# Base added into the accumulators by VectorE between two expert steps, expert bias opens them, embedding gate in eight pieces of 256 columns in odd steps

## The reference

```python
x = _layernorm(DEEPNORM_ALPHA * x + mix, ln1_g[layer], ln1_b[layer], dt)
moe_out = moe(x.reshape(bsz * seq, D_MODEL), router_w[layer], router_b[layer], expert_w_gu[layer],
              expert_b_gu[layer], expert_w_down[layer], expert_b_down[layer]).reshape(bsz, seq, D_MODEL)
ple = jax.nn.sigmoid(x @ ple_gate_w[layer]) * (p[layer] @ ple_proj_w[layer])
x = _layernorm(DEEPNORM_ALPHA * x + moe_out + ple, ln2_g[layer], ln2_b[layer], dt)
...
# in moe, for each expert e of a token's four, with weight g:
#   gate, up = x @ w_gu[e] + b_gu[e];  h = (min(up) + 1) * gate * sigmoid(1.702 * gate);  y += g * (h @ w_down[e] + b_down[e])
```

## Time and profile before

| | us |
|---|---|
| median of 3 runs | 1730.97 (1730.95 to 1731.19) |
| profiled execution, first to last instruction (span) | 1728.9 |
| median of the runs less that span | 2.1 |
| TensorE busy | 1701.2 |
| VectorE busy | 582.5 |
| ScalarE busy | 265.1 |
| mean rate of all transfers | 313 GB/s |

### The profile page before, as it was taken

The page is one execution under the profiler, slowest core; times in us unless marked ns, Lnnn a source line. Parts: engine busy times, 40 slices in busy tenths (PEclk is TensorE's granted clock), DMA queues, the critical chain, the costliest instruction groups (busy, mean ns, idle before and its releaser), DMA issues.

```text
span 1728.9 us, 24503 instructions
## 1 busy us (share of the span) xinstructions
PE 1701.2 (98%) x10237; PEld 1000.7 (58%) x10237; DVE 582.5 (34%) x1085; ACT 265.1 (15%) x455; POOL 26.3 (2%) x37
## 2 busy tenths in 40 slices
PE   9999999999999999999999999999999999999998
PEld 8787888888643433333333343433333338998885
DVE  4685368454331111111111111112121135544643
ACT  1323115002011111101010010101010122112211
POOL 1000000100000000000000000000000000000000
PEclk9999999999999999999999999999999999999999
DMA  9564332545799999999999999999999997443231
GB/s 343 196 257 159 146 123 100 174 164 195 265 405 426 418 425 426 428 427 428 428 428 428 426 428 427 429 426 428 427 429 426 430 394 272 188 154 147 98 141 48
DMA packets 64241, 540.52 MB, mean 313 GB/s; under 512 B 5416, under 2 KB 12360, under 8 KB 34724
## 3 DMA queue, kind: packets, MB, share of 16 engines
q1 hardware_dynamic: 58432, 528.42, 74.4%
q10 hardware_dynamic: 3956, 5.86, 1.2%
q0 software_dynamic: 1776, 5.10, 1.0%
HBM read 533.57 MB, written 5.78 MB: 312 GB/s over the span
## 4 chain that ended last, share of the span: by engine, by line
PE 92%; DMA 5%; DVE 2%; ACT 1%; issue 1%; SPq 0%; DVEq 0%; ACTq 0%
PE small L1482 24%; PE small L1521 12%; PE proj L854 10%; PE proj L1675 7%; PE proj L1038 5%; PE proj L1754 4%; PE proj L1458 3%; PE small L1424 3%; DMA arena<-in_expert_w_gu 3%; PE small L1470 2%; PE small L1117 2%; PE small L1489 2%; PE small L874 2%; PE proj L863 2%; PE small L1621 2%; PE small L1814 2%
## 5 line engine op out<-in xcount | busy, mean ns | idle before, releaser
L1482 PE MATMUL small<-arena 128*64 128x512 f32 x2048 | 446.7, 593 | 3.2 <-DMA arena<-in_expert_w_gu 1.9
L1482 PEld LDWEIGHTS small<-arena 128*64 128x64 f32 x2048 | 151.2, 137 | 282.8 <-issue 275.0
L1521 PE MATMUL small<-arena 128*64 128x512 f32 x1024 | 227.0, 595 | 8.3 <-ACT arena L2010 7.6
L2698 DVE TENSOR_SCALAR arena<-small 128x512 f32<-128x512 f32 x32 | 22.1, 692 | 535.0 <-PE small L1489 535.0
L854 PE MATMUL proj<-arena 128*128 128x256 f32 x832 | 182.9, 380 | 0.0
L854 PEld LDWEIGHTS proj<-arena 128*128 128x128 f32 x832 | 157.2, 190 | 21.8 <-issue 0.5
L1521 PEld LDWEIGHTS small<-arena 128*64 128x64 f32 x1024 | 74.3, 137 | 139.5 <-issue 138.5
L1675 PE MATMUL proj<-arena 128*128 128x128 f32 x1120 | 125.7, 275 | 0.5 <-ACT arena L2087 0.5
L1675 PEld LDWEIGHTS proj<-arena 128*128 128x128 f32 x1120 | 125.3, 192 | 0.7 <-ACT arena L2087 0.7
L2005 ACT ACTIVATE arena<-arena 128x512 f32<-128x512 f32 x32 | 20.2, 631 | 491.6 <-DVE arena L2698 491.6
L1835 ACT ACTIVATE arena<-proj 128x512 f32<-128x512 f32 (+2 forms) x72 | 41.6, 593 | 330.4 <-PE proj L854 130.1
(11 more groups left out here) (454 smaller groups left out, 1539.8 us busy)
## 6 DMA issues: line engine op xcount, KB each, us to landing
arena<-in_expert_w_gu SPq DMA_DIRECT2D x128, 2048.0 KB, 20.3
arena<-in_expert_w_down SPq DMA_DIRECT2D x31, 2048.0 KB, 27.9
arena<-in_expert_w_down SPq DMA_DIRECT2D x33, 1536.0 KB, 30.2
arena<-in_w_in_first SPq DMA_DIRECT2D x20, 2048.0 KB, 8.6
arena<-in_w_in SPq DMA_DIRECT2D x15, 2048.0 KB, 7.4
arena<-in_expert_w_down SPq DMA_DIRECT2D x33, 512.0 KB, 19.7
arena<-in_w_ada SPq DMA_DIRECT2D x6, 2048.0 KB, 12.0
arena<-in_w_branch SPq DMA_DIRECT2D x4, 2048.0 KB, 8.2
```

The costliest lines, as they stand in the source:

```text
L1482: mm = pe.matmul(bank[CAP * half:CAP * half + CAP, :], XG[:, k % 4, k // 4, :], w[:, k % 4, n * D + half * W:n * D + half * W + W], start= ...
L1521: mm = pe.matmul(bank[CAP * half:CAP * half + CAP, :], h[:, m, u, :], w[:, half * W:half * W + W], start=u == 0 and m == 0, stop=u == 1 an ...
```

## The change

Three edits, and the counts of the semaphores that go with them:

- `embed` makes 256 columns at a time, in the odd steps 9 to 23 only, eight pieces instead of sixteen; ScalarE's and VectorE's instructions on a piece are twice as wide and half as many. SGP grows to 256 columns.
- `expert_bias` has no identity matmul any more, and stands in step 1, between `gate_and_up` and `scatter`; its four matmuls open the accumulators (`start=True`), which the first scatter did before.
- VectorE adds `base` into the four accumulators with four tensor additions of 128x512 behind its part of step 25, and TensorE waits for them before step 26.

```diff
             def expert_bias(j):
 
                 for half in range(2):
-                    pe.matmul(acc_bank[2 * j + half][:, :], ident, base[:, j, half * W:half * W + W], start=False, stop=False, skip_group_check=True)
-                    pe.matmul(acc_bank[2 * j + half][:, :], GTT[:, j * P:j * P + P], BD[:, half * W:half * W + W], start=False, stop=False, skip_group_check=True)
+                    pe.matmul(acc_bank[2 * j + half][:, :], GTT[:, j * P:j * P + P], BD[:, half * W:half * W + W], start=True, stop=False, skip_group_check=True)
...
-            def embed(i, j):
+            def embed(n, j):
 
                 for k in range(KD):
-                    mm = pe.matmul(x_bank[:, 0:P], XT[:, k, j * P:j * P + P], PLEW[:, k, bass.ds((i % 8) * P, P)], start=k == 0, stop=k == KD - 1)
+                    mm = pe.matmul(x_bank[:, 0:T], XT[:, k, j * P:j * P + P], PLEW[:, k, bass.ds((2 * n % 8) * P, T)], start=k == 0, stop=k == KD - 1)
                 mm.then_inc(sig("ple_full"), 1)
...
                 if before != 0:
                     if before == 1:
                         pe.wait_ge(sig("proj_out"), proj_no("pp 3") + 1)
+                        for j in range(TT):
+                            expert_bias(j)
                     pe.wait_ge(sig("y_ready"), i)
                     pe.wait_ge(sig("ptw_ready"), i + 1)
-                    scatter(first=before == 1)
+                    scatter()
...
             for j in range(TT):
-                two_steps(8 * j + 8, 8 * j + 16, j)
-            two_steps(24, 26, None, embedded=True)
-            pe.wait_ge(sig("ple_mul"), 18)
-            for j in range(TT):
-                expert_bias(j)
-            two_steps(26, before_two + 1, None)
+                with pe.Fori(4 * j + 4, 4 * j + 8) as n:
+                    expert_step(2 * n, False, embedded=n - 3)
+                    expert_step(2 * n + 1, True, piece=(n, j))
+            two_steps(24, 26, embedded=9)
+            pe.wait_ge(sig("ple_mul"), 10)
+            two_steps(26, before_two + 1)
...
+            with dve.Fori(24, 26) as i:
+                expert_step(i)
+            dve.wait_ge(sig("ptw_full"), 27)
+            for j in range(TT):
+                for half in range(2):
+                    bank = acc_bank[2 * j + half]
+                    do(TTn(bank[:, :], bank[:, :], base[:, j, half * W:half * W + W], ALU.add))
+            dve.nop().then_inc(sig("ple_mul"), 1)
```

More of the change, by code:

```diff
@@ L381, in build @@
         total = room(at, 1).bitcast(I32); at += 4
-        GTT = room(at, T)[2 * EXPERTS:3 * EXPERTS]; at += T
+        GTT, SGP = room(at, T)[2 * EXPERTS:3 * EXPERTS], room(at, T); at += T
         BGU, BD = room(at, D)[0:2 * EXPERTS], room(at, D)[2 * EXPERTS:3 * EXPERTS]; at += D
@@ L386, in build @@
         ln2g, ln2b = LN2[:, 0, :], LN2[:, 1, :]
-        SGP = room(at, P); at += P
         XG = room(at, 4, 2, CAP); at += 512
@@ L736, in _ @@
                 down_second(EXPERTS - 2 + odd, odd, slice(3, 4), last=odd == 1)
-            sp.wait_ge(sig("ple_full"), 16)
+            sp.wait_ge(sig("ple_full"), 8)
             sp.dma_start(ln2g, ins["ln2_g"][0].partition_broadcast(P)).then_inc(sig("ln2_loaded"), 16)
@@ L1450, in _, with scatter @@
             idle_filled()
-            def scatter(tiles_=range(TT), first=False, counted=False):
+            def scatter(tiles_=range(TT), counted=False):
                 for j in tiles_:
@@ L1458, in scatter @@
                         mm = pe.matmul(acc_bank[2 * j + half][:, :], PTW[lo:lo + CAP, j * P:j * P + P], YSB[lo:lo + CAP, :],
-                                       start=first, stop=False, skip_group_check=True)
+                                       start=False, stop=False, skip_group_check=True)
                         if counted:
@@ L1525, in down, with expert_step @@
                 mm.then_inc(sig("y_full"), 1)
-            def expert_step(i, tile, odd, before=None, down_now=True, embedded=False):
+            def expert_step(i, odd, before=None, down_now=True, embedded=None, piece=None):
                 gate_and_up(i)
@@ L1533, in expert_step @@
                         pe.wait_ge(sig("proj_out"), proj_no("pp 3") + 1)
+                        for j in range(TT):
+                            expert_bias(j)
                     pe.wait_ge(sig("y_ready"), i)
                     pe.wait_ge(sig("ptw_ready"), i + 1)
-                    scatter(first=before == 1)
+                    scatter()
                 pe.wait_ge(sig("pick_ready"), i + 2)
[L1538 to L1541, removed]
+                if embedded is not None:
+                    pe.wait_ge(sig("ple_sig"), embedded)
                 gather(x_bank).then_inc(sig("gathered"), 1)
@@ L1550, in expert_step, with two_steps @@
                     down(i, odd, y_bank, HM)
-                if tile is not None:
+                if piece is not None:
                     pe.wait_ge(sig("ple_in"), 32)
-                    embed(i, tile)
-            def two_steps(lo, hi, tile, embedded=False):
+                    embed(*piece)
+            def two_steps(lo, hi, embedded=None):
                 with pe.Fori(lo, hi, 2) as i:
[L1558 to L1565, removed]
-            for j in range(TT):
-                two_steps(8 * j + 8, 8 * j + 16, j)
-            two_steps(24, 26, None, embedded=True)
-            pe.wait_ge(sig("ple_mul"), 18)
-            for j in range(TT):
-                expert_bias(j)
-            two_steps(26, before_two + 1, None)
+                    expert_step(i, False, embedded=embedded)
+                    expert_step(i + 1, True)
+            expert_step(0, False, 0)
+            expert_step(1, True, 1)
+            expert_step(2, False, 2)
+            expert_step(3, True)
+            two_steps(4, 8)
+            for j in range(TT):
+                with pe.Fori(4 * j + 4, 4 * j + 8) as n:
[4 more added lines that the diff above has]
+            two_steps(26, before_two + 1)
             a, b = before_two + 1, before_two + 2
-            expert_step(a, None, False, down_now=False)
+            expert_step(a, False, down_now=False)
             pe.wait_ge(sig("hm_ready"), a + 1)
@@ L2015, in y_copied, with expert_step @@
                 act.activation(YSB, bank[:, :], ACT.Copy).then_inc(sig("y_ready"), 1)
-            def expert_step(i, embed, down_now=True):
+            def expert_step(i, piece=None, down_now=True):
                 sigmoid_of_gate(i)
@@ L2025, in expert_step @@
                     y_copied(i, y_bank)
[L2026 to L2029, removed]
+                if piece is not None:
+                    act.wait_ge(sig("ple_full"), piece - 3)
+                    act.wait_ge(sig("ple_mul"), piece - 3)
+                    act.activation(SGP, x_bank[:, 0:T], ACT.Sigmoid).then_inc(sig("ple_sig"), 1)
             with act.Fori(0, 8) as i:
-                expert_step(i, False)
-            with act.Fori(8, 24) as i:
-                expert_step(i, True)
+                expert_step(i)
+            with act.Fori(4, 12) as n:
+                expert_step(2 * n)
+                expert_step(2 * n + 1, n)
             act.wait_ge(sig("total_ready"), 1)
@@ L2037, in _ @@
             with act.Fori(24, before_two + 1) as i:
-                expert_step(i, False)
+                expert_step(i)
             a, b = before_two + 1, before_two + 2
-            expert_step(a, False, down_now=False)
+            expert_step(a, down_now=False)
             sigmoid_of_gate(b)
@@ L2678, in _, with expert_step @@
             LINKS = 3
-            def expert_step(i, tile, e=None, last=False):
+            def expert_step(i, e=None, last=False, piece=None):
                 link = [0]
@@ L2707, in expert_step @@
                 assert link[0] == LINKS
-                if tile is not None:
-                    dve.wait_ge(sig("ple_sig"), i - 6)
-                    v = base[:, tile, bass.ds((i % 8) * P, P)]
+                if piece is not None:
+                    n, tile = piece
+                    dve.wait_ge(sig("ple_sig"), n - 2)
+                    v = base[:, tile, bass.ds((2 * n % 8) * P, T)]
                     TTn(v, v, SGP, ALU.mult).then_inc(sig("ple_mul"), 1)
             with dve.Fori(0, 8) as i:
-                expert_step(i, None)
+                expert_step(i)
             for j in range(TT):
[L2716 to L2719, removed]
-            before_two = dve.value_load(total[0:1, 0:1], min_val=EXPERTS - 3, max_val=EXPERTS * T // CAP - 3)
[L2721 to L2724, removed]
+                with dve.Fori(4 * j + 4, 4 * j + 8) as n:
+                    expert_step(2 * n)
+                    expert_step(2 * n + 1, piece=(n, j))
+            dve.wait_ge(sig("ple_mul"), 9)
+            do(STT(base, x1, ALPHA, base, ALU.mult, ALU.add))
+            before_two = dve.value_load(total[0:1, 0:1], min_val=EXPERTS - 3, max_val=EXPERTS * T // CAP - 3)
+            with dve.Fori(24, 26) as i:
+                expert_step(i)
```

(6 more changed lines are left out.)

## The result

| | before, us | changed, us |
|---|---|---|
| median | 1730.96 (6 runs, 1730.35 to 1731.19) | 1735.95 (6 runs, 1734.26 to 1738.07) |
| span of the profiled execution | 1728.9 | 1734.4 |

The ratio is 1.0029 with a 95% interval of 1.0019 to 1.0039: the change makes the kernel 5.0 us slower. The profiled execution of the changed kernel took 1736.21 us, 1.8 around its span, and its span grew by 5.5. Another thing stands in the table: the runs of the changed kernel lie 3.8 us apart, those of before 0.8.

What follows compares the result with a forecast made beforehand. The prediction took the stream of expert weights, at its ceiling of 428 GB/s, as the bound. Embedding 0, base 0 and bias +2.7 on 1731.0 gave 1733.7 us, with 8 in 10 for 1730.5 to 1735.4.

Steps and rivals of the forecast that it cites:

- what bounds the kernel: Expert steps: the weight stream at 427 to 428 GB/s, 29.4 us an expert, sets the end in the second half.
- The faster rival: Whole kernel: TensorE is the bound and its work counts, so time falls by 9.1 us to 1721.9; chance 0.12.
- the base through VectorE: Seam between steps 25 and 26: 8.4 us off TensorE, VectorE's four additions hidden beside the down block; worth 0.
- the gate in eight pieces: Steps 8 to 23: TensorE does 4.9 us less, but the weights set the path; worth 0.
- the bias in step 1: Between gate-and-up and scatter: 4.2 us of matmuls delay transfers, less a 1.5 us store; +2.7 us.
- its own signs of being wrong: Middle rate above 430 GB/s, last landing not moved by 2 to 4 us, or TensorE waiting at the seam for VectorE.
- The store: Transfer queue at the gap before 576.97 us: 8.8 − 7.3 = 1.5 us of waiting work absorbs part of TensorE's delay.
- no store at the gap: At the 8.8 us transfer: small rows ahead explain its time, so the whole delay passes, +4.2, 1735.2 us; chance 0.15.
- The clock: Granted clock: not at risk, as it reads 1.00 in the window with the 1.24 us wait; cost 0.
- The price of the matmuls: Step 1: four bias matmuls at 1.05 us each as at the seam, 4.2 us; lower bound 3.4.
- Is there something for the queue to do meanwhile?: At 542 to 560 us: yes, since the last gate-and-up transfer takes 18.7 us to land and carries a store.
- the first rival: Same as The faster rival: whole kernel, TensorE the bound, 1721.9 us; decided by a stream of 441 GB/s or more; chance 0.12.

Runs made afterwards that it cites:

- the bias late: The changed kernel with the four bias matmuls behind step 25 and the first scatter opening the accumulators again: 1731.00 us, ratio 0.9999.
- the bias between the quarters: The changed kernel with one bias matmul behind each quarter of gate-and-up of step 1 instead of four in a row: 1735.69 us, ratio 1.0027.
- 128 rows: The changed kernel with the four opening matmuls of step 1 made with 128 rows (identity with x1), bias not computed: 1734.58 us, ratio 1.0020.
- half bias: The changed kernel with two of the four bias matmuls kept in step 1 and two between steps 5 and 6: 1732.56 us, ratio 1.0011.
- the last variants: Changed kernel, bias between steps 5 and 6: 1731.72 us; also expert 4's first down half issued earlier: 1731.05; that with bias in step 7's quarters: 1731.26; kernel before, that transfer: 1730.32.
- the one with the lowest median: The kernel before with only the first half of expert 4's down weights issued ahead of its gate and up: 1730.32 us, ratio 0.9993.
- the transfer ahead: The changed kernel with the first half of expert 4's down weights issued ahead of its gate and up: 1733.39 us, ratio 1.0015.

## Why the prediction was right or wrong

**Right: what bounds the kernel.** The end of the expert phase is set by the stream of weights at 427 to 428 GB/s, and the same TensorE work removed as in the changed kernel, with the bias late, gives nothing: 1731.0. The faster rival is gone. **Right: the base through VectorE at nothing**, four additions in 2.89 us (0.70 each, priced at 0.69) beside a down block of 7.09. **Right: the gate in eight pieces at nothing.** TensorE began to wait for weights in step 9 instead of about 16, and waited 10.2 us in sum instead of 13 to 14, which changed no time.

**Right in kind, too small in size: the bias in step 1**, +2.7 predicted, +5.0 measured, from three errors in that one term. Two made it too small and one too large. Of its own signs of being wrong one came true: the last landing moved by 5.6 us and not by 2 to 4.

- *The store, taken at 1.5 us.* "The store at that moment is thus only 8.8 − 7.3 = 1.5 us" failed: a delay of 1.8 us cost 1.4 to 1.9, so the store is 0 to 0.4 us. The place was right. It is the one with the smallest store, and it settles what arrives at the end. The rival "no store at the gap" had this right, and the low rate of 573 to 600 was the sign for it. Its reason, that the 8.8 us came from the small rows ahead and not from a full queue, was not tested by itself.
- *The clock, taken at nothing.* "The clock isn't at risk by the rows" failed: 1.6 us in the profiled execution, 1.4 in the median. I looked at the clock where TensorE waits; it fell while TensorE was busy. No row of before shows four matmuls of 32 rows in a row, so its rows could not say that the clock was safe, and the term wanted an upper bound.
- *The price of the matmuls, taken at 4.2 us.* 3.63 were measured, near the lower bound of 3.4. The 1.05 us at the seam was the price of a matmul of 32 rows between ones of 128; in a row of its own kind it is 0.9. The kernel with the bias between the quarters shows the same 1.06 again.

"Is there something for the queue to do meanwhile? At 542 to 560 us yes" was too generous as well, though it took nothing from the sum. The place did run dry, at 545 to 555 us. The 18.7 us belongs to a transfer issued behind the down weights of 542.68 and 546.11, which are themselves held back. Even the transfer of 542.68 misleads: it took 11.4 us, 4.1 over the 7.3 of an empty queue, but at a delay of 4.0 (128 rows) the place had already lost 1.3 us.

With the three in their measured sizes the sum is 3.6 + 1.4 − 0 = +5.0 us. The range ended at 1735.4 since the rival with no store was worked out with 4.2 us and without the clock; without the fallen clock the time would have lain inside it (1734.6, with 128 rows).

Two workings do not fit with the rest, and neither enters the sum. By the earlier trace rows the gate in eight pieces saves 8 x (2 x 2.11 − 3.65) = 4.6 us and not 4.9. And the first rival asks for a stream of 441 GB/s, where the paragraph ahead of it takes 435 as enough. The slices of the changed kernel stay at 430 or below too.

Not settled: why the clock falls in some executions and not in others; what made the half bias's longest run long; and what of the 0.7 us between the last variants is real. A kernel that is faster beyond doubt wasn't found; the one with the lowest median lies 0.8 us under the kernel before.

## What to carry to other kernels

Where one stream of transfers runs at its ceiling to the end of a phase, the time is decided before it fills: a delay there is lost but for the store of the thinnest place behind it. Here that place held nothing and the delay cost its whole length, while work placed behind it was nearly free in both directions.

A store read from landings (the time of a transfer less that of a lone one) was too large at both places here: 1.5 us where 0 to 0.4 were, and 4.1 where 2 to 3 were (estimates, from the half bias, the 128 rows and the transfer ahead). Take it as an upper bound, look for the thinnest place and not the first, and test it with a delay of a known length, as the half bias did, together with the rate in narrow windows. To fill a place that isn't the thinnest should give nothing back; no run here tried that.

Matmuls that use few rows of the array are best put where time is free, since behind a row of them the clock may fall, which cost up to 1.7 us for each 3.4 us that it lasted. Kept apart they had no such fall in any trace, but the four cost 4.7 us instead of 3.6.

## What the runs showed of the hardware

- The granted clock fell from 2.4 to 1.2 GHz while TensorE was busy without a gap, behind four matmuls of 32 rows in a row: for 3.4 us in three traces and 6.8 in one, while two traces with the same four had no fall. With 128 rows in the same place the runs lay 0.7 us apart instead of 3.8. The Trainium skill, page "TensorE: Matmul & The Clock Gate", Part 1, ties the clock to how busy the engine was. The busy share of the trace was 1.00 here, so that share did not tell of these falls.
- A matmul of 32 rows and 512 columns took 0.9 us behind its like and 1.06 us between matmuls of 128 rows. With 128 rows it took the same 0.9 us behind its like.
- A VectorE addition of 128x512 with one operand and the output in a matmul bank took 0.70 us, as long as one that only reads such a bank (0.69).
- A 2048 KB transfer into a nearly empty queue landed in 7.3 us in the expert steps (issued at 582.60), the same as the best elsewhere.
